# A hybrid decoder trunk on one core: the order of a unit's block sums, one tile fewer in front of the units, and six matrix steps moved

## What is computed

```
h = x + 1/2 * SwiGLU_a(RMSNorm(x))        # first feed-forward
... GLA heads and S5 heads, w_out, cross attention ...
h = h + 1/2 * SwiGLU_b(RMSNorm(h))        # second feed-forward

def swiglu(x, w_gu, w_down):              # w_gu 1024 x 5632, w_down 2816 x 1024
    g, u = jnp.split(x @ w_gu, 2, axis=-1)
    return (jax.nn.silu(g) * u) @ w_down
```

## Time and profile before

| | |
|---|---|
| median of 3 runs | 1295.68 us (1295.6 to 1296.47) |
| the profiled execution's own time | 1296.79 us |
| its span | 1295.0 us, granted clock 0.997 |
| PE busy | 1270.0 us (98%), 10275 matmuls |
| DVE busy | 861.3 us (67%) |
| ACT busy | 527.3 us (41%) |
| POOL busy | 350.0 us (27%) |
| chain that ended last | PE 89%, DVE 6%, ACT 2% |
| DMA | 129.95 MB, mean 100 GB/s |

### The profile page before, as it was taken

The page is one execution under the profiler, slowest core; times in us unless marked ns, Lnnn a source line. Parts: engine busy times, 40 slices in busy tenths (PEclk is TensorE's granted clock), DMA queues, the critical chain, the costliest instruction groups (busy, mean ns, idle before and its releaser), DMA issues.

```text
span 1295.0 us, 24300 instructions
## 1 busy us (share of the span) xinstructions
PE 1270.0 (98%) x10275; PEld 1230.6 (95%) x10275; DVE 861.3 (67%) x1056; ACT 527.3 (41%) x797; POOL 350.0 (27%) x409
## 2 busy tenths in 40 slices
PE   7999999999999999999999999999999999999997
PEld 6999999999999999999999997599999999999997
DVE  4987379844789736558565537478895589637952
ACT  6544145521223422565443224246453255414543
POOL 0025623276896202000002100032230133102321
PEclk9999999999999999999999999999999999999998
DMA  6232233263213442125423656322233323223221
GB/s 185 81 89 82 82 98 98 82 131 88 83 55 85 90 91 63 53 66 153 120 83 97 203 204 225 133 82 79 84 96 85 98 82 99 83 83 96 86 62 73
DMA packets 227148, 129.95 MB, mean 100 GB/s; under 512 B 22240, under 2 KB 221392, under 8 KB 227024
## 3 DMA queue, kind: packets, MB, share of 16 engines
q1 hardware_dynamic: 223168, 123.37, 33.4%
q10 hardware_dynamic: 3872, 5.04, 1.1%
HBM read 121.42 MB, written 5.78 MB: 98 GB/s over the span
## 4 chain that ended last, share of the span: by engine, by line
PE 89%; DVE 6%; ACT 2%; issue 2%; DMA 0%; SPq 0%; DVEq 0%; ACTq 0%
PE PS L723 86%; PE PS L1315 1%; DVE wl L1967 1%; DVE xl L2076 1%; DMA AR<-in_x_prompt 0%; PE PS L791 0%; ACT wh L1453 0%; DVE PS L2055 0%; ACT gua L1599 0%; DVE PS L2221 0%; DVE Hs L2376 0%; PE PS L1401 0%; DVE gua L2151 0%; PE PS L1293 0%; PE PS L933 0%
## 5 line engine op out<-in xcount | busy, mean ns | idle before, releaser
L1453 ACT ACTIVATE wh<-raw 128x1024 fp32r<-128x1024 f32 (+1 forms) x128 | 132.2, 1033 | 377.0 <-PE PS L723 376.9
L723 PE MATMUL PS<-yh,wh 128*128 128x288 f32 x960 | 206.1, 296 | 2.5 <-DVE yl L2164 1.6
L723 PE MATMUL PS<-yl,wh 128*128 128x288 f32 x960 | 205.0, 295 | 0.0
L723 PE MATMUL PS<-yh,wl 128*128 128x288 f32 x960 | 205.0, 295 | 0.0
L1967 DVE TENSOR_TENSOR wl<-raw,wh 128x1024 fp32r<-128x1024 f32 (+1 forms) x128 | 160.1, 1251 | 62.6 <-ACT wh L1453 61.3
L723 PE MATMUL PS<-xh,wh 128*128 128x288 f32 x768 | 171.7, 305 | 0.3 <-DVEq L2146 0.2
L723 PE MATMUL PS<-xh,ARr 128*128 128x288 f32 x768 | 169.5, 296 | 0.3
L723 PE MATMUL PS<-xh,wl 128*128 128x288 f32 x768 | 164.9, 297 | 0.0
L723 PE MATMUL PS<-xl,wh 128*128 128x288 f32 x768 | 164.8, 296 | 0.0
L723 PEld LDWEIGHTS PS<-yh,wh 128*128 128x128 f32 x960 | 154.0, 188 | 4.2 <-DVE yl L2164 1.8
L723 PEld LDWEIGHTS PS<-yh,wl 128*128 128x128 f32 x960 | 154.3, 188 | 0.0
(11 more groups left out here) (370 smaller groups left out, 2217.0 us busy)
## 6 DMA issues: line engine op xcount, KB each, us to landing
raw<-in_w_ffn_gu SPq DMA_DIRECT2D x88, 512.0 KB, 3.9
raw<-in_w_ffn_down SPq DMA_DIRECT2D x32, 512.0 KB, 4.0
raw<-in_w_in SPq DMA_DIRECT2D x16, 512.0 KB, 4.1
raw<-in_w_ckv SPq DMA_DIRECT2D x16, 512.0 KB, 3.9
raw<-in_w_ffn_down SPq DMA_DIRECT2D x16, 384.0 KB, 3.4
Hs<-in_cache_mem_k SPq DMA_DIRECT2D x6, 1024.0 KB, 7.0
raw<-in_w_out SPq DMA_DIRECT2D x8, 512.0 KB, 4.0
raw<-in_w_cq SPq DMA_DIRECT2D x8, 512.0 KB, 5.1
```

The lines of the kernel that those rows point to most:

```text
L723: return e.matmul(out, lhsT, rhs, start=start, stop=stop, **kw)
L1453: e.activation(wh[:, n % 2, 0:K * P], raw[:, n % 4, 0:K * P], ACT.Copy).then_inc(w_hi, 1)
```

## The change

Three things. In the list of every unit DVE makes S1, S2 and S4 of the next unit in a row, then `low_last`, then S3; the counts on `sum_ok` follow (`high_sums` waits for three sums, `high_last` for four). The first feed-forward has three plain tiles and five units in its first group in place of four and four, and DVE's, ACT's and PE's lists in front of the units are drawn together accordingly: two conversions fall away, `tokens_low` for chunks 6 and 7 and the first `low_sums` come before the eviction of the last plain block. In the second feed-forward `low_sums` also comes before that eviction. And six of the matrix steps are done behind the last three down blocks in front of the third group (two behind each), the other twelve of the former eighteen one by one behind each block of the third group.

```diff
--- before.py
+++ after.py
@@ -218,7 +218,7 @@
         ROWS = dict(prompt=(1, 2, 4, 5), decode=(3, 6))
         EXPS = dict(prompt=(4, 8, 13, 17), decode=(9, 18))
         TURNS = dict(prompt=(1, 2, 3, 5), decode=(4, 6))
-        HK, PLAIN = KD // 2, {(1, 0): 4, (2, 0): 2, (1, 2): FGROUPS[2]}
+        HK, PLAIN = KD // 2, {(1, 0): 3, (2, 0): 2, (1, 2): FGROUPS[2]}
         xg = view(MM, 7168, HK, T)
         tok_h, tok_l = view(ARr, 0, HK, 4, TH), view(ARr, 8 * T, HK, 4, TH)
         tok_hf, tok_f = tok_h.bitcast(F32), view(AR, 8 * T, HK, 4, TH)
@@ -899,7 +899,7 @@
             dense(2, 0, KD, xh, xl, inside=(spread_roots, 0), ahead=True)
             dense(3, 1, KD, xh, xl)
             parameters_turn()
-            for n in range(4, 8):
+            for n in range(4, 6):
                 dense(n, n % 2, KD, xh, xl)
             seven_group(0)
             seven_group(1, within=s5_turn)
@@ -1496,7 +1496,7 @@
 
             def high_sums(v):
 
-                e.wait_ge(S("sum_ok"), 4 * v + 4)
+                e.wait_ge(S("sum_ok"), 4 * v + 3)
                 if v >= 2:
                     e.wait_ge(S("pr_done"), 7 * v - 9)
                 e.activation(operands(v, S1, 3, 0), sums124, ACT.Copy).then_inc(S("hi_ok"), 1)
@@ -1504,7 +1504,7 @@
             def high_last(v):
 
                 n = units[v] + 1
-                e.wait_ge(S("sum_ok"), 4 * v + 3)
+                e.wait_ge(S("sum_ok"), 4 * v + 4)
                 if v:
                     e.wait_ge(S("pr_done"), 7 * v)
                 if v in (0, FIRST_FFN2):
@@ -1648,16 +1648,12 @@
             conv(5)
             tokens_high(5)
             hidden(1, 3, 1, groups[0])
-            conv(6)
             tokens_high(6)
+            high_gate(0)
             hidden(2, 4, 0, groups[0])
-            conv(7)
             tokens_high(7)
+            high_sums(0)
             hidden(2, 5, 1, groups[0])
-            high_gate(0)
-            hidden(3, 6, 0, groups[0])
-            high_sums(0)
-            hidden(3, 7, 1, groups[0])
             e.wait_ge(S("t_lo"), HK)
             e.wait_ge(S("lam_mm"), 2)
             seven_group(0)
@@ -2119,11 +2115,11 @@
 
                 nxt, going = after(v), v not in FIRST_UNIT
                 if nxt:
-                    sum_of(S1, nxt)
+                    for j in (S1, S2, S4):
+                        sum_of(j, nxt)
                 low_last(v)
                 if nxt:
-                    for j in (S2, S3, S4):
-                        sum_of(j, nxt)
+                    sum_of(S3, nxt)
                 else:
                     conv(units[v] + 2)
                 if going:
@@ -2181,7 +2177,7 @@
                         conv(n + 2)
                     if i in (0, 2, 3):
                         if b == KD - 3:
-                            for j in (S1, S2, S3, S4):
+                            for j in (S1, S2, S4, S3):
                                 sum_of(j, v + 1)
                         elif b == KD - 2:
                             low_sums(v + 1)
@@ -2189,6 +2185,9 @@
                         second_half_low()
                     if within and b == 4:
                         within()
+                    elif within and b > 4:
+                        matrix_step(2 * b - 10)
+                        matrix_step(2 * b - 9)
 
             def parameters_turned():
 
@@ -2226,9 +2225,7 @@
             def third_group(i, n, par):
 
                 plain_low(i, n, par, groups[4])
-                matrix_step(3 * i + par)
-                if par:
-                    matrix_step(3 * i + 2)
+                matrix_step(6 + 2 * i + par)
 
             def third_down(i, n, par):
 
@@ -2269,7 +2266,11 @@
                     conv(1)
             conv(2)
             rms(0)
-            for n in range(8):
+            for n in range(6):
+                if n == 5:
+                    for k in (6, 7):
+                        tokens_low(k)
+                    low_sums(0)
                 e.wait_ge(mm_done, seq(n) + 3)
                 hidden(n // 2, n, n % 2, groups[0])
                 if n != 1:
@@ -2280,17 +2281,16 @@
                 elif n == 1:
                     for k in range(HK):
                         tokens_low(k)
-                elif n < 6:
+                elif n < 4:
                     tokens_low(n + 2)
-                elif n == 7:
-                    low_sums(0)
                 plain_low(n // 2, n, n % 2, groups[0])
-                if 0 < n < 5:
+                if 0 < n < 4:
                     token_sums(n + 3)
                 if n == 3:
                     parameters_turned()
-                elif n == 6:
-                    for j in (S1, S2, S3, S4):
+                    token_sums(7)
+                elif n == 4:
+                    for j in (S1, S2, S4, S3):
                         sum_of(j, 0)
             seven_group(0)
             seven_group(1, within=s5_turned)
@@ -2686,15 +2686,15 @@
                     rms(3)
                     conv(n + 2)
                     tokens_low(KD - 1, base=KD)
+                if b == 3:
+                    low_sums(FIRST_FFN2)
                 e.wait_ge(mm_done, seq(n) + 3)
                 hidden(i, n, b % 2, g)
                 if b:
                     conv(n + 2)
-                if b == 3:
-                    low_sums(FIRST_FFN2)
                 plain_low(i, n, b % 2, g)
                 if b == 2:
-                    for j in (S1, S2, S3, S4):
+                    for j in (S1, S2, S4, S3):
                         sum_of(j, FIRST_FFN2)
             for i in range(2, 5):
                 seven_group(i)
```

## The result

The changed kernel takes 1326.99 us (median of 4 runs, 1326.43 to 1328.89) beside 1295.74 us for the kernel before on the same chip: a ratio of 1.0241, interval [1.0225, 1.0257], slower by 31 us. The profiled execution has a span of 1324.5 us, 29.5 more than before, at a granted clock of 0.995.

What follows compares the result with a forecast made beforehand. PE bounds the kernel, with DVE next to no room; after the change DVE sets the pace. Terms -1.6 + 15.8 + 4.5 + 8.9 + 4.6 - 1.4 = +30.8 us on the median 1295.68 give 1326.4 us, range 1301 to 1332.

Steps and rivals of the forecast that it cites:

- Step 2: New order in units: POOL holds low_last and S3; further units stall 1.71 us; groups of eight +7.9 each, last +4.5.
- everything else: All places outside the listed groups and fronts: nothing else moves, 0 us.
- The 0.15 us: In a unit, low_last becomes ready about 0.15 us after POOL's L666 starts, so it stands until L666 ends.
- Rival A: In units, low_last gets in before L666; stalls begin some units later; +6.5 us, 1302.2 us; chance 0.14.
- the main case: In units, low_last is held by L666 and L663 goes before S3; 1326.4 us, own range 1318 to 1332; chance 0.64.
- p: Phase: end of DVE's multiply L2139 of the unit before, counted from the unit's first matmul; -0.16 in the unit read.
- The front of the first feed-forward: First S1 product stalls 5.55 us, unit 1 2.5, units 2 and 3 1.71 each: +8.9 us.
- The 2.5 us of unit 1: First feed-forward: DVE leaves unit 0 at p = 1.2, so unit 1 stalls 2.5 us.
- The front of the second: Second feed-forward: the 1.7 and 0.6 us waits go, units 1 to 4 stall 7.1 us: +4.6 us.
- The matrix steps: Six moved before the third group cost nothing in DVE's idle time; waits there shrink: -1.4 us, between 0 and -2.7.
- B: Faster: the order fills DVE's 0.66 us idle time, POOL does no harm; 1287.6, or 1293.2 with the front stall; chance 0.18.
- C: No change: 15 units with a stall of some 0.2 us would just eat up the 8 us gain; chance 0.04.

Runs made afterwards that it cites:

- order_only: The kernel before with only the order of the sums changed (S1, S2, S4, low_last, S3, with matching counts): 1321.83 us, ratio 1.0200.
- the two memsets: The kernel after with one POOL operation replaced by a memset of the same operand: L666 in one run (1296.84 us), L663 in the other (1294.41 us).
- order_mid: The kernel after with the unit's order S1, S2, low_last, S4, S3, two sums ahead of low_last in place of three: 1296.57 us, ratio 1.0001.
- four_mid: The kernel before (four plain tiles, its own front) with order_mid's units, the change's early sums of the second feed-forward and its matrix steps: 1292.77 us, ratio 0.9972.
- three_early: order_mid with mid_step's moved steps, tokens_low of 6 and 7 after low_sums, and unit 0's PSUM sums and high_sums earlier: 1290.11 us, ratio 0.9962.
- mid_step: order_mid with the last six matrix steps of the third group's down blocks one block later: 1295.46 us, ratio 0.9991.
- a11_memset: The kernel after with POOL's L663 (low part of A11 and A12) replaced by a memset of its output: 1294.41 us, ratio 0.9985.
- three_keep: three_early with ACT's first keep of unit 0 moved ahead of block 5's high part and the wait for tokens' low parts: 1290.71 us, ratio 0.9957.
- order_back: The kernel after with the old order in every unit (S1, low_last, S2, S3, S4) and the old counts: 1299.76 us, ratio 1.0030.

## Why the prediction was right

**The unit.** Step 2 held to the hundredth where it could be read: `low_last` ended 3.69 us after the gate multiply, S3 6.49, L2101 7.16 (7.15 foreseen), and the round was 12.86 us. The stalls were 1.06 in the third unit of a group and 1.61 in each further one, 0.1 below the 1.71 forecast. Groups of eight lost 8.1 us each (7.9), the last 4.6 (4.5). That step alone carries two thirds of the result, and order_only, the two memsets and order_mid show its mechanism from four sides.

**The nearness of the total is in part luck.** The terms miss by -2.3, +1.9 and -1.2 us (first front, matrix steps, everything else) and partly cancel: 30.8 forecast, 29.5 between the two profiled spans. The median rose by 31.3 all the same, as the profiled execution of before was 1.1 us above its median and that of the kernel after 0.6 below.

**The 0.15 us.** Rival A hung on them, and `low_last` did get in first in five units that make sums for a next one, in a way that neither the main case nor A had: it did not come earlier, L666 came later. ACT's L1512, ahead of L1514 and L666, also waits until PE is through with the unit before. Where DVE is well ahead of PE, that wait ends last. ACT in unit 2 of the second feed-forward, whose gate multiply before it ended at 951.81:

```profile
953.25 0.63 ACT L1512 ACTIVATE xh<-AR 128x512 fp32r<-128x512 f32 x1 [0.66 <-PE PS L723]
```

L666 started there at 954.49, 2.68 us behind the gate multiply, `low_last` at 953.92. In the second unit of each group that follows down blocks L666 came 2.91 us behind. The prediction put p at -0.23 after that unit without a working; its own round of 12.86 us would have given +0.31 and 1.6 us of stall in the third unit. The -0.24 and the 1.06 measured are what the row of an unheld `low_last` gives. In unit 1 of the first feed-forward it was a matter of 0.02 us: `low_last` at 78.68, L666 at 78.70.

**The front of the first feed-forward**, forecast +8.9 - 1.6, measured +5.0. The stall itself was 5.5 us, as worked out. The clock did fall: PE ran at half clock from 62.84 for 6.8 us, of which it worked from 65.91 on, with matmuls 0.240 us apart in place of 0.133. That cost (69.67 - 65.91) x (1 - 0.133 / 0.240) = 1.7 us, the value that I had left in the range. But it was no loss on top: unit 0 took 18.4 us, and DVE, which the clock does not slow, came out of it at p = -0.52 in place of the 1.2 forecast. So even a held `low_last` would have cost unit 1 some 0.8 us and not 2.5, and as it got in first, there was no stall. The 2.5 us of unit 1 is the term that was mis-sized: it was worked out for the full clock, and added to a range that had the clock's fall in it, although the one takes from the other. The two units behind stalled 1.5 and 1.6. These terms give 5.5 + 3.1 + 1.7 - 2.55 - 1.6 = +6.1; unit 0 also began at 58.8, 0.7 us earlier than 72.29 - 12.8 (not traced further), and some 0.4 us stay unexplained.

**The front of the second**, forecast +4.6, measured +4.4, of which 1.1 is the slower down blocks, so 3.3 by its own terms: stalls of 2.0, 1.06 and 1.61, and 3.4 us of half clock behind the 2.0 us one, which I had not foreseen. Unit 1 took 14.8 us, 11.15 + 2.0 and 1.6 for the clock; the unit behind it began with p = -1.19 and had no stall, so here too the clock's cost and the stall that it took away nearly cancel.

**The matrix steps**, forecast -1.4, measured +0.5, the sign wrong. The step that failed reads "so they cost nothing". I had looked for DVE's idle time, and it was there: no eviction of those down blocks is late. What I had not asked was what the steps do to POOL, which shares with them what it shares with `low_last`. They held its tables back by 6.8 us, and the tables' last operation then met a step in the down blocks. The two gains came as forecast (0.26 us of the `yl` wait for 0.4, and the `wl` wait with its 0.16), and the two new waits of 0.58 and 1.06 us ate them.

**B, C.** The 0.66 us of idle time before `low_last` was filled as B says, and with order_mid in its place nothing is lost to POOL; then B's end comes true in part, 1292.8 in four_mid and 1290.1 in three_early. Which of the two operations starts first is the point at which it decided. C's sum was wrong in itself: 15 stalls of 0.2 us are 3 us, and eating up the 8 takes 0.5 each.

## What to carry to other kernels

When an operation on DVE with two SBUF inputs is moved by a few tenths of a microsecond, look at where POOL's operations start, not only at DVE's idle time: a meeting costs the rest of POOL's operation, and a second such operation behind it costs POOL's next one too. Operations with a PSUM input are the ones to lay beside POOL's; those with two SBUF inputs belong ahead of it. The same holds the other way round: filling DVE's idle time next to POOL's work makes POOL late, so follow POOL's list to its end and see what it meets there.

## What the runs showed of the hardware

- When DVE's held operation ends and both engines have a next one ready, POOL goes next: S3 stood 2.1 us in the units of the kernel after in which `low_last` was held (2.77 us in place of 0.69). A DVE operation that was queued directly behind another did not keep POOL out.
- A memset on POOL, which reads no SBUF, holds nothing: `low_last`, started inside one, took 0.68 us. The Trainium skill ("SBUF — State Buffer", SBUF: two separate sides) has a two-input DVE operation contend only with a POOL operation that reads SBUF, and this agrees.
- A POOL operation with one SBUF input does hold DVE, but not to its recorded end: L655 is recorded with 5.77 us, and in the kernel after, in order_mid and in mid_step the held DVE operation went on 3.9 us after its start (417.11 - 1.34 - 411.86; 407.08 - 1.34 - 401.82; 406.42 - 0.96 - 401.58). The same section has the shared port held for the whole instruction. By these rows either the hold ends at two thirds of the instruction or the instruction ended before its recorded end; POOL's recorded spans are rough, and no run here tells the two apart. For planning, the 3.9 us count.
- The granted clock of PE fell to 1.2 GHz with the front stalls of 5.5, 3.8 and 3.5 us (a11_memset) and behind one of 2.02 us (at 946.9 in the kernel after). It stayed at 2.4 GHz behind one of 2.06 us in three_early, one of 1.96 in three_keep and behind all of 1.6 us and less, of which the kernel after has fourteen of about that length. So of two stalls of 2.0 us one was followed by a fall and one was not. The same front stall was followed by 6.8 us at the lower level in some kernels (the kernel after, order_mid) and by 3.4 in others (mid_step, order_back).
- The same 48 matmuls of a down block took 6.24 us in some kernels and 6.40 in others, at a granted clock of 1.00 in both; in the first group of each feed-forward it was one or the other for the whole of the group's down blocks. The cause is open. Look at this before a difference of 1 us is put down to a change.
